# Moving three low-part subtractions on VectorE in a one-core hybrid attention and FFN layer

## What is computed

```python
proj = x @ w_in[l]
o_a = dsa_attention(...)             # top-128 keys by an indexer, softmax
o_b = chunk_rel_attention(...)       # chunked softmax with relative bias
o_c = window_sink_attention(...)     # sliding window, grouped queries, sinks
o_d = stick_breaking_attention(...)  # a = exp(log_sigmoid(z) + reverse cumulative sum of log_sigmoid(-z))
y = sum over i of sigmoid(gate_i) * (branch_i @ w_branch[l, i])
x = layer_norm(ALPHA * x + y @ w_out[l], ...)
hg, hu = jnp.split(x @ w_ffn_in[l], 2, axis=-1)
x = layer_norm(ALPHA * x + (silu(hg) * hu) @ w_ffn_out[l], ...)
```

## Time and profile before

| | before |
|---|---|
| median of 3 runs | 842.61 us |
| profiled execution | 842.3 us |
| its span, first to last instruction | 840.5 us |
| PE busy | 829.5 us (99%) |
| DVE busy | 509.4 us (61%) |
| ACT busy | 353.4 us (42%) |
| granted TensorE clock, mean | 0.998 |

### The profile page before, as it was taken

How to read it: one execution, slowest core, us unless ns; L and a number is a source line. 1 busy time by engine, 2 the same in 40 slices (tenths; PEclk the granted TensorE clock), 3 DMA queues, 4 the chain that set the end, 5 groups by cost and what they waited for, 6 DMA issues and landing times.

```text
span 840.5 us, 10290 instructions
## 1 busy us (share of the span) xinstructions
PE 829.5 (99%) x3943; PEld 692.6 (82%) x3943; DVE 509.4 (61%) x861; ACT 353.4 (42%) x557; POOL 29.2 (3%) x75
## 2 busy tenths in 40 slices
PE   9999999999999999999999999999999999999996
PEld 6888889788888888888888988888888888888885
DVE  5559899887789888685653976433333433222237
ACT  6554656785555536525422732222222222211122
POOL 1700000000000000000000001000000000000000
PEclk9999999999999999999999999999999999999999
DMA  8352123112121221222262214222222222222202
GB/s 276 124 210 96 51 100 101 51 51 101 60 92 63 88 101 51 101 101 74 76 249 102 96 55 156 97 98 100 100 100 100 100 100 101 100 101 101 100 1 101
DMA packets 15816, 84.51 MB, mean 101 GB/s; under 512 B 1808, under 2 KB 3860, under 8 KB 7072
## 3 DMA queue, kind: packets, MB, share of 16 engines
q1 hardware_dynamic: 13472, 76.89, 25.5%
q0 software_dynamic: 2016, 6.86, 2.3%
q10 hardware_dynamic: 288, 0.20, 0.1%
HBM read 81.82 MB, written 2.13 MB: 100 GB/s over the span
## 4 chain that ended last, share of the span: by engine, by line
PE 85%; DVE 10%; ACT 2%; issue 1%; DMA 1%; SPq 0%; DVEq 0%; ACTq 0%
PE bank L1356 57%; PE bank L1595 19%; PE bank L1658 2%; PE bank L1519 2%; DVE sel L959 2%; DVE w_all L882 2%; PE bank L1506 2%; PE bank L1403 1%; DVE top L957 1%; DVE probsT L1061 1%; ACT w_all L539 1%; PE bank L1481 1%; PE bank L1483 1%; DVE probs L1064 1%; DVE probs L1048 1%
## 5 line engine op out<-in xcount | busy, mean ns | idle before, releaser
L1356 PE MATMUL bank<-x_hi,w_all 128*128 128x512 f32 x1424 | 342.5, 390 | 0.0
L1356 PEld LDWEIGHTS bank<-x_hi,w_all 128*128 128x128 f32 x1424 | 266.1, 188 | 54.9
L882 DVE TENSOR_TENSOR w_all<-raw,w_all 128x2048 fp32r<-128x2048 f32 x65 | 148.9, 2290 | 124.6 <-ACT w_all L539 101.9
L1356 PE MATMUL bank<-x_lo,w_all 128*128 128x512 f32 x712 | 180.8, 391 | 0.0
L1356 PEld LDWEIGHTS bank<-x_lo,w_all 128*128 128x128 f32 x712 | 132.2, 188 | 26.6
L539 ACT ACTIVATE w_all<-raw 128x2048 fp32r<-128x2048 f32 x45 | 86.4, 1920 | 94.6 <-PE bank L1595 85.5
L1595 PE MATMUL bank<-w_all,h_hi 128*128 128x512 f32 x352 | 96.7, 389 | 0.0
L1595 PEld LDWEIGHTS bank<-w_all,h_hi 128*128 128x128 f32 x352 | 66.0, 188 | 13.8 <-DVE w_all L1291 0.2
L1595 PE MATMUL bank<-w_all,h_lo 128*128 128x512 f32 x176 | 56.8, 389 | 0.0
L821 ACT ACTIVATE h_hi<-swi 128x512 f32 (+1 forms) x22 | 13.9, 633 | 94.2 <-DVE swi L1268 94.2
L558 ACT ACTIVATE gates<-bank 128x512 f32<-128x512 f32 x30 | 17.9, 598 | 71.5 <-PE bank L1356 64.0
(11 more groups left out here) (285 smaller groups left out, 925.2 us busy)
## 6 DMA issues: line engine op xcount, KB each, us to landing
raw<-in_stream SPq DMA_DIRECT2D x67, 1024.0 KB, 4.8
resid<-in_x POOLq DMA_DIRECT2D x1, 2048.0 KB, 10.4
xraw<-in_xT SPq DMA_DIRECT2D x6, 256.0 KB, 5.3
out<-result SPq DMA_DIRECT2D x3, 512.0 KB, 2.6
early_raw<-in_stream SPq DMA_DIRECT2D x1, 1024.0 KB, 8.7
bias_b<-bias_vectors POOLq DMA_DIRECT2D x1, 1024.0 KB, 8.2
bias_a<-bias_vectors POOLq DMA_DIRECT2D x1, 1024.0 KB, 12.0
ln_g<-in_g POOLq DMA_DIRECT2D x2, 512.0 KB, 7.8
```

Of the source, the lines that this page charges most:

```text
L882: dve.tensor_tensor(lo, raw[:, s, :], hi.bitcast(f32), ALU.subtract).then_inc(lo_ready, 1)
L1356: ins = pe.matmul(dst, lhs[a](k), rhs[b](k), start=n == 0, stop=n == n_all - 1)
```

## The change

It has three parts, all on DVE, with one wait on PE that follows from the third.

1. In slot 12, the last one with a D unit, the low part of chunk 13 is no longer the first instruction of the slot but stands behind the scan, the subtractions and `stack_low`. In slots 8 and 10, which a late slot follows, it stays.
2. In the late slots 7, 9 and 11 the round between `stack_low` and `probs_low` goes behind `probs_low`; the first round and the low part of chunk t + 1 stay ahead.
3. The low part of the second FFN chunk is made in two instructions, one for each tile of 128 columns: the first where it was, the second behind `x1_low` of the second half. PE's tile 0 waits for the first, tile 1 for the second.

```diff
+        def by_column_tile(w):
+
+            return w.rearrange("p (k j n) -> p k j n", k=KT, j=2)
...
-                    if t > 1 and t != PAIR + 1:
+                    if t > 1 and t != PAIR + 1 and (kind is None or late(t + 1)):
                         low(t + 1)
...
                     if late(t):
-                        search(first_round, 1)
                         probs_low(before)
-                        search(first_round + 1, 3)
+                        search(first_round, 4)
                         first_round, rounds = first_round + 4, rounds - 4
...
                     stick_scan(now)
                     stack_low(UNIT_AT.get(t + 1))
+                    if t > PAIR + 1 and not late(t + 1):
+                        low(t + 1)
...
             def ffn_pair(p, parity, first=False, early=False):
-                low(2 * p + (FIN0 + 1), (FIN0 + 1) % 2)
                 if first:
+                    dve.wait_ge(hi_ready, FIN0 + 1)
+                    hi, lo = [by_column_tile(w) for w in parts_of(FIN0 + 1)]
+                    source = by_column_tile(raw[:, (FIN0 + 1) % 2])
+                    dve.tensor_tensor(lo[:, :, 0, :], source[:, :, 0, :], hi[:, :, 0, :].bitcast(f32),
+                                      ALU.subtract).then_inc(fin_half_ready, 1)
                     x1_turned(1)
                     x1_low(1, 0, KT)
+                    dve.tensor_tensor(lo[:, :, 1, :], source[:, :, 1, :], hi[:, :, 1, :].bitcast(f32),
+                                      ALU.subtract).then_inc(lo_ready, 1)
+                else:
+                    low(2 * p + (FIN0 + 1), (FIN0 + 1) % 2)
...
                     if n == KT + KT // 2:
-                        if which == 0 and half == 0:
-                            pe.wait_ge(fin_half_ready, 1)
+                        if which or half == 0:
+                            pe.wait_ge(fin_half_ready, which + 1)
                         else:
-                            pe.wait_ge(lo_ready, FIN0 + which)
+                            pe.wait_ge(lo_ready, FIN0)
...
                     x1_tiles(1, 1, (0,))
+                    pe.wait_ge(lo_ready, FIN0 + 1)
                     products(banks[3][:], columns(home(FIN0 + 1), P, P, CW), x_all, range(KT)).then_inc(up_done, 1)
```

## The result

| | before | after |
|---|---|---|
| median of 9 runs each | 842.67 us | 844.55 us |
| ratio, 95% interval | | 1.0026 [1.0018, 1.0035] |
| range of the runs | 842.24 to 843.78 us | 844.05 to 846.44 us |
| span of the profiled execution | 840.5 us | 842.2 us |
| mean granted TensorE clock | 0.998 | 0.996 |

The change costs 1.9 us. The prediction was +0.9 us with a range to 844.5; the time lies just above it, on the side of its third rival. The execution that was profiled is the fastest of the nine.

A forecast was written before the change was run, and what follows sets the result against it. It took ScalarE and VectorE to set the time from 60.84 to 163.52 us, and TensorE afterwards. Parts 1 to 3, +1.45 + 0.0 - 0.55 = +0.9 us, gave 843.5 us against the median, range 842.2 to 844.5.

The forecast's parts named there:

- third rival: TensorE's clock falls in the second of two close waits, slots 12 to 13: +2.5 to +4.1 us, chance 0.05.
- Part 1, the early scan: Slot 12: the first scan starts near 157.75 instead of 158.59, after the first logarithm, a gain of 0.84 us.
- Part 1, the wait: Slot 13: TensorE waits for chunk 13's moved subtraction and starts at 166.5 instead of 165.06, 1.45 us later.
- Part 2: Late slots: TensorE gains 0.9 us but waits 0.9 us longer in slot 12, worth 0.0 us.
- One sign that the prediction names against itself: The prediction is wrong if the chain before 163 us is already TensorE's.
- Part 3: First FFN pair: TensorE's wait in the second half's first sixteen products goes, -0.55 us.
- the 1.95 among the prediction's signs: In the new profile the sixteen products of the FFN's second half should take 1.95 us.
- its term for TensorE's clock: Slots 12 and 13: no clock cost in the sum; a fall only as a rival, 1.6 or 3.2 us, chance 0.05.
- The sign of this rival: Products in slot 13 are 0.45 us apart.
- The sum: Whole kernel: +1.45 + 0.0 - 0.55 = +0.9 us, 843.5 us against the median.
- The prediction's bounds: Whole kernel: the bounds of the three parts taken together, +0.2 to +2.2 us.
- an early relu that gives the scan nothing: Slot 12: upper bound of part 1's term, the scan starts no earlier, 0.84 us more.

The follow-up runs named there:

- e1: Part 1 of the change alone on the kernel before: 843.74 us against 842.32.
- e2: Part 2 of the change alone on the kernel before: 842.53 us against 842.32.
- e9: The kernel of e10 with part 2 undone, one search round again ahead of `probs_low` in late slots: 840.68 us against 842.29 for the kernel before.
- e10: The kernel of e6 plus chunk 13's high part made by ScalarE in slot 11, a repeat run: 839.41 us against 842.29 for the kernel before.
- e3: Part 3 of the change alone on the kernel before: 841.75 us against 842.32.
- e4: Parts 2 and 3 on the kernel before, without part 1: 841.94 us against 842.41.
- e8: The whole change, with TensorE waiting for chunk 13's low part only at slot 13's 17th product: 842.49 us against 842.41 for the kernel before.
- e6: The kernel of e8 with chunk 13's subtraction moved behind `probs_low` on VectorE: 841.16 us against 842.41 for the kernel before.
- e5: The whole change plus eight unneeded TensorE products before slot 13's wait for the low part: 843.00 us against 842.32 for the kernel before.

## Why the prediction was right or wrong

- **Part 1, the early scan.** Right. The scan was to start near 157.75; it starts at 157.60, in an execution whose chain is 0.14 us earlier (the Abs at 154.35 for 154.49), and it waits for the logarithm.
- **Part 1, the wait.** The mechanism was right, its size 0.2 us too high: 166.5 was forecast, 166.33 measured with the same 0.14 put back. The subtraction started 0.61 us behind the second stack, not 0.7, and TensorE 0.06 us behind its end, not 0.15. Nothing queued behind it made a second wait, as worked out. e1 prices the wait by itself at 1.1 us (its runs with the clock up), where 1.2 was expected.
- **Part 2.** Right: 0.0 us, by e2 in the median (+0.2, interval across 1), because the chain of the earlier trace rows is not TensorE's there. e9 and e10 show that this was the reason. One sign that the prediction names against itself did appear: the chain printed for the changed kernel runs through TensorE up to 151.5 and enters ScalarE only at 151.75. ScalarE's own rows speak against that path: it waits 3.30 us for VectorE's addition, and the instruction at 151.75 follows the one that waited without a gap.

```profile
151.09 0.63 ACT L659 ACTIVATE o_hi<-o_sum_D 64x512 fp32r<-64x512 f32 x1 [3.30 <-DVE o_sum_D L973]
...
151.75 0.60 ACT L568 ACTIVATE v_abd<-bank 128x512 f32<-128x512 f32 x1
```

- **Part 3.** Right: -0.55 us was forecast, and it is -0.54 in the change, in e3 and in e4. (The sixteen products take 2.08 us in the row; the 1.95 among the prediction's signs is nearer to a count by their starts, 16 x 0.12 = 1.92.)
- **The clock.** Here the prediction failed. The step that failed is its term for TensorE's clock: the sum and the range put it at nothing, and the third rival, which has the mechanism, got a chance of 0.05. The ground was the one wait of 1.1 us that the trace before shows harmless, but the change makes 1.5 and 1.9 us with 1.07 us of work between, three times as much, and no row spoke for a clock that holds through that. What the runs showed in its place is a clock that falls to 0.50 and costs 1.37 us in slot 13, where the prediction priced the fall at 1.6 to 3.2. The sign of this rival came: eight products in slot 13 are 0.41 us apart on average (166.19 to 169.49). Its total of +2.5 to +4.1 us was too high for the +1.9 measured. The Trainium skill that the prediction cites (TensorE: Matmul & The Clock Gate, Part 1) says that idle drops the engine to 1.2 GHz and work earns 2.4 back, and the trace after agrees with it: granted clock 0.50 from 166 to 169, 1.00 from 170 on. How likely a fall is at waits of this size, only the runs say.
- **The sum.** With the measured terms, 1.27 + 1.37 - 0.54 is +2.10 us. The two profiled executions differ by +1.75: the 0.14 us by which the later one's chain happened to be early and the 0.21 us of scatter between slot 13 and the FFN make the difference. The medians differ by +1.88. The prediction's bounds, +0.2 to +2.2, would have held that number, but by luck: their upper end stood for an early relu that gives the scan nothing, and the scan did gain. (The lower end is added up wrongly: 1.15 - 0.2 - 0.6 is +0.35.)

## What to carry to other kernels

An instruction that is taken from the front of the critical engine's queue must be asked for its own due time and for what then stands behind it: here a 2.3 us subtraction was moved to save 0.84 us and became the next thing that TensorE waited for, and only when both the wait (e8) and the order behind it (e6) were moved too did the early scan pay (e6: -1.25 us, of which part 3 is -0.54). A wait on TensorE that grows to 1.9 us or more, as in e1, e2 and e4, is priced with the clock, 1.4 to 1.6 us on top, at least as a chance. Where work on TensorE that nobody needs fits into the wait, it can be cheaper than the idle time (e5). And an engine's gain ahead of a place where another chain sets the time is worth nothing until that chain is shortened, and its full size afterwards (e2 against e9 and e10).

## What the runs showed of the hardware that was not expected

The granted clock did not follow the length of a wait alone. In the profiled executions it held after one wait of 1.15 us (before), after one of 2.30 us (e2) and after two of 1.4 us with 3 us of work between (e8); it fell after 1.49 and 1.86 us with 1.1 us of work between (the change), after 0.30 and 1.86 us (e1), and after one of 2.28 us (e4), which is e2's case over again. Where it fell it was at 0.50 for about 3 us and cost 1.4 to 1.6 us: from the start of slot 13 to its scores 3.53 us (the change) and 3.70 (e1) for 2.16, and in e4, where the transposes were slow too, 4.86 us from their start to the scores for 3.23. By the mean clocks of the runs one program falls on either side from run to run: they are at 0.995 or 0.996 in three of the eleven runs of e1, in two of e2 and in three of e4, and the traces of e1 and e4 are of such runs. What decides between the two outcomes is left open: no run here varies it alone.
